# A mixture-of-experts decoder step: the last expert's activations transposed inside the preceding expert's down projection

## The reference, cut to what matters

```python
def moe(x, router_w, router_bias, w_gate, w_up, w_down):
    ...                                  # scores, top-1 group, top-2 experts of it
    for e in range(N_EXPERTS):           # 16 experts
        h = jax.nn.silu(xt @ w_gate[e]) * (xt @ w_up[e])      # 1024 -> 512
        y = y + combine[:, e:e + 1] * (h @ w_down[e])         # 512 -> 1024
    return y.reshape(shp)
```

## Time and profile before

| | us |
|---|---|
| median of 3 runs (1504.57 to 1505.84) | 1504.78 |
| the profiled execution | 1503.68 |
| its span, from first to last instruction | 1501.9 |
| TensorE busy | 1258.5 (84% of the span) |
| VectorE busy | 998.2 (66%) |
| ScalarE busy | 716.0 (48%) |
| GpSimd busy | 227.5 (15%) |

### The profile page before, as it was taken

One profiled execution on the slowest core, in us unless ns is written; L12 is line 12 of the kernel. 1 busy time (PEld: TensorE's weight loads), 2 busy tenths in 40 slices (PEclk: granted clock), 3 DMA queues, 4 the chain that ended last, 5 costly groups with the idle time before them and its releaser, 6 DMA issues.

```text
span 1501.9 us, 18000 instructions
## 1 busy us (share of the span) xinstructions
PE 1258.5 (84%) x6469; PEld 1011.3 (67%) x6469; DVE 998.2 (66%) x1458; ACT 716.0 (48%) x963; POOL 227.5 (15%) x272
## 2 busy tenths in 40 slices
PE   4999978889998599999994279987995899999940
PEld 4989877775445478888883179943454788888830
DVE  2766354442245599999993932738445999999938
ACT  2533222221012388888872342264122888888822
POOL 3101242211100110000002300136001101000023
PEclk9999989996698699999997589998986999999985
DMA  6120060010525489999963702020444899999733
GB/s 191 57 85 29 1 208 1 1 33 17 172 94 196 158 320 421 410 414 414 408 271 128 226 29 85 1 112 3 175 160 162 318 415 417 414 410 415 288 134 104
DMA packets 63069, 296.59 MB, mean 197 GB/s; under 512 B 6608, under 2 KB 32937, under 8 KB 50720
## 3 DMA queue, kind: packets, MB, share of 16 engines
q1 hardware_dynamic: 51104, 252.77, 43.6%
q0 software_dynamic: 7296, 26.22, 4.9%
q10 hardware_dynamic: 4608, 16.78, 2.8%
HBM read 268.86 MB, written 26.89 MB: 197 GB/s over the span
## 4 chain that ended last, share of the span: by engine, by line
PE 78%; DVE 13%; issue 3%; ACT 3%; POOL 2%; DMA 2%; POOLq 0%; DVEq 0%; ACTq 0%
PE bank L1026 23%; PE bank L1056 12%; PE bank L950 6%; PE bank L612 4%; PE bank L613 4%; PE bank L640 4%; PE bank L641 3%; PE bank L937 3%; PE bank L1016 2%; PE bank L1149 2%; PE bank L961 1%; DVE X L1881 1%; PE bank L599 1%; PE bank L1044 1%; PE bank L836 1%
## 5 line engine op out<-in xcount | busy, mean ns | idle before, releaser
L1174 ACT ACTIVATE GU_HIGH<-work 128x1024 fp32r<-128x1024 f32 x256 | 270.1, 1060 | 64.6 <-PE bank L1026 64.6
L1026 PE MATMUL bank<-GU_HIGH,XGT_HIGH 128*128 128x512 f32 x512 | 205.4, 401 | 13.3 <-DVE XGT_LOW_B L2029 13.3
L2053 DVE TENSOR_TENSOR WUP_LOW<-work,GU_HIGH 128x1024 fp32r<-128x1024 f32 x128 | 153.7, 1222 | 15.2 <-ACT GU_HIGH L1174 10.6
L2053 DVE TENSOR_TENSOR WGT_LOW<-work,GU_HIGH 128x1024 fp32r<-128x1024 f32 x128 | 155.6, 1223 | 12.0 <-ACT GU_HIGH L1174 3.7
L2060 DVE TENSOR_TENSOR WDN_LOW<-work,WDN_HIGH 128x1024 fp32r<-128x1024 f32 x128 | 152.0, 1222 | 8.0 <-ACT WDN_HIGH L1174 3.6
L1174 ACT ACTIVATE WDN_HIGH<-work 128x1024 fp32r<-128x1024 f32 x128 | 135.3, 1062 | 44.1 <-PE bank L1056 44.1
L1174 ACT ACTIVATE work<-bank 128x512 f32<-128x512 f32 (+4 forms) x148 | 59.5, 445 | 132.0 <-PE bank L694 29.6
L1026 PEld LDWEIGHTS bank<-GU_HIGH,XGT_HIGH 128*128 128x128 f32 x512 | 98.4, 192 | 34.1 <-DVE XGT_LOW_B L2029 14.5
L1174 ACT ACTIVATE W_HIGH<-work 128x1024 fp32r<-128x1024 f32 x36 | 38.0, 1057 | 150.7 <-PE bank L613 80.7
L1056 PE MATMUL bank<-WDN_HIGH,HT_HIGH 128*128 128x512 f32 x256 | 103.8, 405 | 2.8 <-DVE HT_LOW L2040 2.8
L1026 PE MATMUL bank<-WGT_LOW,XGT_HIGH 128*128 128x512 f32 x256 | 102.5, 400 | 0.0
(11 more groups left out here) (446 smaller groups left out, 2943.1 us busy)
## 6 DMA issues: line engine op xcount, KB each, us to landing
work<-in_moe_w_gate_dram SPq DMA_DIRECT2D x32, 2048.0 KB
work<-in_moe_w_up_dram SPq DMA_DIRECT2D x32, 2048.0 KB, 10.2
work<-in_moe_w_down_dram SPq DMA_DIRECT2D x32, 2048.0 KB, 9.5
y_rows<-work ACTq DMA_DIRECT2D x32, 512.0 KB
work<-in_ab_w_in_dram SPq DMA_DIRECT2D x10, 1024.0 KB, 5.3
work<-in_c_w_in_dram SPq DMA_DIRECT2D x8, 1024.0 KB, 9.1
x_rows<-X SPq DMA_DIRECT2D x8, 512.0 KB, 2.6
work<-in_c_w_out_dram SPq DMA_DIRECT2D x1, 4096.0 KB, 13.0
```

The costliest lines, as they stand in the source:

```text
L1026: last = mm(psum, x, w, start=(k == m == 0), stop=(k == KD - 1 and m == 2))
L1174: return nc.scalar.activation(out, in_, ACT.Copy, scale=scale)
L2053: V.tensor_tensor(low[u][:, 2 * n:2 * n + 2, :], w[u][:, 2 * n:2 * n + 2, :], high, ALU.subtract)\
```

## The change

The last two down projections of a layer, with the transposes of the last expert, are replaced by one function `last_downs` on TensorE, and ScalarE and VectorE get their last step written out to match. The transposes of expert 15 stand between steps f = 1 and f = 2 of expert 14's down projection and write bank 4. Their rounded part goes into the first half of `XGT_HIGH` and the remainder into `XGT_LOW_A`. The down projection of 15 reads those and writes banks 0 and 2. Every other step of the layer is as before.

```diff
+            def last_downs(g):
+
+                pe.wait_ge(ht_ready, g)
+                pe.wait_ge(y1_out, g - 1)
+                for f in (0, 1):
+                    down_part(0, g - 1, f, HT_HIGH, HT_LOW, (7, 6))
+                pe.wait_ge(h_ready, g + 1)
+                for f in range(4):
+                    last = tr(heads_of(4)[:, f, :], every(HB[1], FF // P, f), ident[:, :])
+                last.then_inc(h_ps, 1)
+                for f in (2, 3):
+                    down_part(0, g - 1, f, HT_HIGH, HT_LOW, (7, 6))
+                pe.wait_ge(ht_ready, g + 1)
+                for f in range(4):
+                    down_part(1, g, f, XGT_HIGH, XGT_LOW_A, (0, 2))
...
                 up(l, 8, 1, base + 15)
-                down(l, 0, base + 14)
-                h_transposed(1, base + 15)
-                down(l, 1, base + 15)
+                last_downs(base + 15)
...
-                step(NE // 2 - 1, 0, 13, False)
-                h_rounded(base + 15)
-                store(0, base + 14, 14)
-                result(8, 1, base + 15)
-                store(1, base + 15, 15)
+                g = base + 15
+                round_units("up", 8, 1, g)
+                store(1, g - 2, 13)
+                h_rounded(g - 1)
+                silu(1, g)
+                round_down(8, 1, g, (0, 1))
+                act.wait_ge(h_ps, g + 1)
+                copy(XGT_HIGH[:, 0:4, :], heads_of(4)).then_inc(ht_high, 1)
+                round_down(8, 1, g, (2, 3))
+                result(8, 0, g - 1)
+                store(0, g - 1, 14)
+                result(8, 1, g, 0)
+                store(1, g, 15)
...
-                step(NE // 2 - 1, 0, False)
-                h_split(base + 15)
-                result(8, 1, base + 15)
+                g = base + 15
+                split_units("up", 1, g)
+                h_split(g - 1)
+                h_product(1, g)
+                split_down(1, g, (0, 1))
+                dve.wait_ge(ht_high, g + 1)
+                V.tensor_tensor(XGT_LOW_A[:, :, :], heads_of(4), XGT_HIGH[:, 0:4, :].bitcast(F32), ALU.subtract).then_inc(ht_ready, 1)
+                split_down(1, g, (2, 3))
+                result(8, 0, g - 1)
+                result(8, 1, g, 2)
```

More of the change, by code:

```diff
@@ L1045, in h_transposed, with down_part @@
                 last.then_inc(h_ps, 1)
+            def down_part(u, g, f, high, low, banks):
+                pe.wait_ge(down_split, 4 * g + (f + 1))
+                for half in (1, 0):
+                    cols = slice(512 * half, 512 * half + 512)
+                    for n, (x, w) in enumerate(((high, WDN_HIGH), (high, WDN_LOW[u]), (low, WDN_HIGH))):
+                        last = mm(bank[banks[half]][:, :], x[:, f, :], w[:, f, cols],
+                                  start=(f == n == 0), stop=(f == 3 and n == 2))
+                last.then_inc(down_used, 1)
             def down(l, u, g):
@@ L1051, in down @@
                 for f in range(4):
[L1052 to L1058, removed]
+                    down_part(u, g, f, HT_HIGH, HT_LOW, (7, 6))
+            def last_downs(g):
[12 more added lines that the diff above has]
+                    down_part(1, g, f, XGT_HIGH, XGT_LOW_A, (0, 2))
             def experts(l):
@@ L1402, in round_units, with round_down @@
                         copy(GU_HIGH[(2 * UNITS * u + first + n) % 4][:, :, :], w[u][:, 2 * n:2 * n + 2, :]).then_inc(gu_rounded, 1)
-                def round_down(pairs, u, g):
+                def round_down(pairs, u, g, some=range(4)):
                     act.wait_ge(down_in[u], arrivals(l, pairs))
-                    for f in range(4):
+                    for f in some:
                         at_least(act, down_used, 4 * g + (f - 3))
@@ L1414, in silu, with result @@
                     nc.scalar.activation(SG[u], bank[u][:, :], ACT.Silu).then_inc(sg_done, 1)
-                def result(pairs, u, g):
+                def result(pairs, u, g, b=7):
                     act.wait_ge(down_used, 4 * g + 4)
                     at_least(act, y_stored[u], arrivals(l, pairs - 1))
-                    copy(YO[u][:, 0:512], bank[7][:, :]).then_inc(y0_out, 1)
+                    copy(YO[u][:, 0:512], bank[b][:, :]).then_inc(y0_out, 1)
                 def store(u, g, e):
@@ L1425, in store, with step @@
                        .then_inc(y_stored[u], 16)
-                def step(i, v, before, more=True):
+                def step(i, v, before):
                     u, g = (1 + v) % 2, i * 2 + (base + 1 + v)
@@ L1434, in step @@
                     silu(u, g)
-                    if more:
-                        round_units("gate", i + 2, 1 - u, g + 1)
-                        x_rounded(g + 1)
+                    round_units("gate", i + 2, 1 - u, g + 1)
+                    x_rounded(g + 1)
                     round_down(i + (v + 1), u, g)
@@ L2040, in h_split, with result @@
                     V.tensor_tensor(HT_LOW[:, :, :], heads_of(7), HT_HIGH[:, :, :].bitcast(F32), ALU.subtract).then_inc(ht_ready, 1)
-                def result(pairs, u, g):
+                def result(pairs, u, g, b=6):
                     dve.wait_ge(down_used, 4 * g + 4)
                     at_least(dve, y_stored[u], arrivals(l, pairs - 1))
-                    V.tensor_copy(YO[u][:, 512:1024], bank[6][:, :]).then_inc(y1_out, 1)
+                    V.tensor_copy(YO[u][:, 512:1024], bank[b][:, :]).then_inc(y1_out, 1)
                 def split_units(which, u, g, some=range(UNITS)):
@@ L2054, in split_units, with split_down @@
                             .then_inc(gu_split, 1)
-                def split_down(u, g):
-                    for f in range(4):
+                def split_down(u, g, some=range(4)):
+                    for f in some:
                         dve.wait_ge(down_rounded, 4 * g + (f + 1))
```

## The result

The changed kernel took 1496.28 us (median of 4 runs, 1494.92 to 1497.71), the kernel before 1505.31 us beside it. The ratio is 0.9943 with a 95% interval of 0.9929 to 0.9956, so 8.6 us faster (6.6 to 10.7). Forecast were 1495.1 us and 9.7 us. A copy of the changed kernel, in five more rounds, gave 1496.67 us and the same ratio.

What follows compares the result with a forecast made beforehand. An uncovered TensorE stall before expert 15's down projection, plus layer 0's lowered clock, was taken as the loss. Savings of 6.11 us (layer 0) and 3.57 (layer 1) make 9.68; 1504.78 - 9.68 = 1495.1 us, range 1492.6 to 1498.0.

Steps and rivals of the forecast that it cites:

- What bounds the stretch: Expert 14's first down matmul to VectorE's last result copy: bank 7 holds back the transposes, an uncovered 3.80 us stall.
- TensorE's stream: Expert 14's and 15's down matmuls 0.227 us apart, transposes 0.49 us between them; 11.57 us without a wait.
- new wait for `h_ready`: TensorE's wait for expert 15's product, midway through expert 14's down projection: 1.8 us to spare, costs nothing.
- The join: Start of expert 15's down projection: TensorE waits 0.1 us for its operands in each layer, bounds 0 to 0.5.
- Slices and stores: Later down slices keep their margins, the third 1.6 us; expert 14's store ends 801.9, expert 15's starts 802.4, no overlap.
- The sum of the stretches: Both layers' ends shrink to 11.67 us: 6.11 us saved in layer 0, 3.57 in layer 1, together 9.68.
- the clock's 2.55 us: Layer 0, expert 15's down projection: 8.30 us against 5.75 in layer 1, lost to the lowered clock, counted as gain.
- a later clock change moves: Rival, 9%: everything after layer 0 runs 6 us earlier, a clock change elsewhere costs 2.55 us, giving 1497.6 us.
- From the last result copy to the next layer's first matmul nothing should change: Expected profile sign: behind VectorE's last result copy, the time to the next layer's first matmul stays as before.
- the two stretches have shrunk and a later one has grown: Sign of being wrong: both layers' ends get shorter, but a later part of the kernel gets longer.

Runs made afterwards that it cites:

- late remainder: Changed kernel with VectorE's remainder behind the last two `WDN_LOW` slices instead of ahead of them; 1503.89 us, ratio 0.9992 to the kernel before.
- layer 1 alone: The change made in layer 1 only, layer 0 keeping the old order of the kernel before; 1501.16 us, ratio 0.9979.
- own banks: Changed kernel's buffers and banks, but transposes behind all of expert 14's down projection, rounding and remainder behind all four slices; 1502.12 us, ratio 0.9994 to the kernel before.
- stall filled: Kernel before with 7 unread matmuls ahead of expert 15's transposes and 5 behind them, in both layers; 1503.35 us, ratio 0.9992.
- Layer 0 alone: The change made in layer 0 only, layer 1 keeping the old order of the kernel before; 1501.42 us, ratio 0.9984.

## Why the prediction was right, point by point

- **What bounds the stretch.** Right in the chain and in what the new order saves. The reason given, bank 7, is the smaller part: with the banks alone 0.8 of the 3.6 us a layer went, the rest with the order. With one VectorE instruction in the wrong place 1.2 of the 8.6 us timed were left (-0.3 to 2.6).
- **TensorE's stream.** Matmul distance 0.227, transposes 0.49 forecast, 0.48 measured (793.37 to 794.30 less 2 x 0.227). The new wait for `h_ready` cost nothing: the product ended 1.8 us ahead of the transposes.
- **The join.** 0.1 us taken as waiting, 0 to 0.5 as bounds. TensorE did not wait: the remainder ended at 796.71, 0.1 us before TensorE's next matmul at 796.82. The 0.1 us came in the 23 distances behind it, 5.31 us (796.82 to 802.13) where 5.21 were taken, so this term had the right size in the wrong place. The prediction had seen such an excess after the old wait, 0.14 us, and put it under the bounds.
- **Slices and stores.** No wait for a late slice. Expert 14's store was issued at 800.03 and takes about 2.6 us, expert 15's at 803.33, so they did not meet.
- **The sum of the stretches.** 11.67 us forecast for each; 11.68, 11.64, 11.67, 11.66, 11.65 and 11.68 measured. The two shrank by 9.70 us in the profiles, 9.68 forecast.
- **The term that was mis-sized: the clock's 2.55 us.** They are real in the stretch, and frequent: in layer 0 four of six executions with a stall of 3 to 3.8 us left unfilled had the fall (the kernel before three times, the late remainder once; not layer 1 alone and not own banks), in layer 1 none of six. That the fall prefers one layer I had not seen; I had treated it as the same luck in both. And it is not a full gain: executions with the fall took about 1.9 us less before layer 1's stretch. From the start of layer 0's stretch to the start of layer 1's, the three executions of before take 642.14, 642.47 and 642.38 us, the three with the change in layer 0 take 637.90, 638.39 and 638.52. The difference of the means is 4.06 us, not 6.11. With 3.6 of layer 1 this makes 7.7 us, within the measured 6.6 to 10.7, but by the traces about 2 of the 9.7 us in the sum were not there. That the forecast still held is luck in part: its range of 1492.6 to 1498.0 us takes in a gain of 7.7 as well as one of 9.7. My rival "a later clock change moves" had 9% and 2.55 us; in part it is what happened. All three executions with the change in layer 0 lack the rise of the clock in the last transposes, but so do two with the old order there (layer 1 alone, stall filled), so the shift is not shown to be what decides.
- **The signs.** "From the last result copy to the next layer's first matmul nothing should change" holds as far as the last transposes of layer 0's norm, 52.05 us behind the copy in both kernels. The sign "the two stretches have shrunk and a later one has grown" came true, by 1.3 us in those transposes and the small ones.
- **The profiled execution.** Its own gain of 6.93 us is 6.10 + 3.60 less 1.86 between the stretches and 0.93 ahead of them, 6.91.

The Trainium skill (TensorE: Matmul & The Clock Gate, Part 1) says that the windows of the clock's watching run freely, so that the point of change varies from run to run. The traces agree only in part: layer 0's stall had the fall in three executions of the kernel before, at 17.8 to 18.0 us each, and escaped it in one with the same code there (15.23).

**Still open.** Layer 0 alone was timed 2.4 us faster (0.9 to 3.8), while its trace says about 4.1. Its eleven runs spread widely (1497.8 to 1503.7), so a second group may be in them that one profile doesn't show. The two layers alone add up to 5.6 us and both together give 8.6; the intervals overlap, but nothing here explains the difference. Nor is it shown why the clock returns during the transposes at 860 us in five executions and not in five others; a fall ahead is not what it takes. Of the difference in between only two pieces are in rows here, and the places vary: layer 1's first gate takes 8.52 us in the changed kernel and 7.84 in its copy, against 7.56 before.

## What to carry to other kernels

When a loop is software-pipelined, look at its last iteration: the step that normally hides under the next iteration's work has nothing to hide under there, and buffers that are idle by then can be lent to it. Giving it its own buffers is the smaller part; its pieces must also stand early enough in every engine's list. A saving worked out instruction by instruction can be exact and still not be the saving in time, because the clock can change elsewhere further on: count a stall in full, and the clock's part only after a run in which TensorE's waits are filled.

## What the runs showed of the hardware

A stall of 3.8 us with 0.72 us of TensorE work in it lowers the granted clock from the 2.4 to the 1.2 GHz level in some places and not in others (0.50 against 1.00 behind it). With twelve useless matmuls in it, or ten small ones, the clock stayed at 1.00 in both layers in the one execution profiled of each (stretches 15.24 to 15.28). Left unfilled it fell in four of six executions in layer 0. More is to be had elsewhere: extra matmuls in the waits around the first gates made the kernel 6.0 us faster, and in five waits 12.4 us (1496.67 to 1484.27), more than the change itself. They cost time where they outlast the wait, 0.45 and 0.99 us ahead of the first projection.
